# Where the second block's modulation vectors are summed: beside the first expert stage on VectorE, or partly by TensorE in 32-column tiles

## The reference, cut to what matters

```
mod = silu(c_2) @ ada_w_2 + ada_b_2            # (1024) @ (1024 x 6144)
sh1, sc1, gt1, sh2, sc2, gt2 = split(mod, 6)
xn   = rmsnorm(h, mix_norm_g) * (1 + sc1) + sh1
proj = xn @ w_in                               # queries, kv latent, index, shift and gate columns
...                                            # attention and a recurrent mixer
h = h + gt1 * (merged @ w_out)
xn2 = rmsnorm(h, moe_norm_g) * (1 + sc2) + sh2
h = h + gt2 * experts(xn2)                     # 32 experts, two per token
```

## Time and profile before

| | |
|---|---|
| time, median of 3 runs | 1485.1 us (1484.5 to 1487.49) |
| the profiled execution: its time, and its span | 1484.08 us, 1482.3 us |
| TensorE busy (matmul) | 1160.5 us, 78% of the span |
| VectorE, ScalarE, GpSimd busy | 36%, 18%, 3% |
| mean DMA rate over the span | 274 GB/s, 405.72 MB moved |
| first expert stage, first gate product to last down product | 258.6 to 514.8 us |

### The profile page before, as it was taken

One profiled execution on the slowest core, in us unless ns is written; L12 is line 12 of the kernel. 1 busy time (PEld: TensorE's weight loads), 2 busy tenths in 40 slices (PEclk: granted clock), 3 DMA queues, 4 the chain that ended last, 5 costly groups with the idle time before them and its releaser, 6 DMA issues. The chain is left out here.

```text
span 1482.3 us, 17064 instructions
## 1 busy us (share of the span) xinstructions
PE 1160.5 (78%) x6643; PEld 688.1 (46%) x6643; DVE 529.3 (36%) x1312; ACT 260.9 (18%) x654; POOL 41.6 (3%) x100
## 2 busy tenths in 40 slices
PE   2799688998899979788999997867666576566656
PEld 2688536443343347466777776543221221222212
DVE  5369573232233320665744446233011011010111
ACT  1233202111111220323522220011100100101000
POOL 0000000000000020000011100000000000000000
PEclk9999795999999979888999997878887887878888
DMA  9667954799999773022101101753999999999995
GB/s 346 233 253 263 413 191 183 296 428 426 427 430 427 298 270 118 17 98 74 57 2 57 58 16 44 281 234 139 421 422 422 422 422 422 422 422 422 422 421 232
DMA packets 78635, 405.72 MB, mean 274 GB/s; under 512 B 14231, under 2 KB 15444, under 8 KB 45812
## 3 DMA queue, kind: packets, MB, share of 16 engines
q1 hardware_dynamic: 78580, 404.98, 67.9%
HBM read 403.92 MB, written 1.05 MB: 273 GB/s over the span
## 5 line engine op out<-in xcount | busy, mean ns | idle before, releaser
L1049 PE MATMUL ps<-ring,hT_sb 128*32 128x512 f32 x768 | 117.0, 766 | 72.4 <-DMA ring<-in_expert_w_gate 42.1
L1412 PE MATMUL ps<-ring,hT_sb 128*64 128x512 f32 x448 | 117.6, 609 | 7.3 <-DMA ring<-in_expert_w_gate 5.5
L1049 PEld LDWEIGHTS ps<-ring,hT_sb 128*32 128x32 f32 x768 | 28.7, 136 | 154.4 <-issue 91.8
L1049 PE MATMUL ps<-side,hT_sb 128*32 128x512 f32 x256 | 42.6, 826 | 36.3 <-DMA side<-in_expert_w_up 18.5
L529 PE MATMUL ps<-hT_sb,ring 128*128 128x256 f32 x256 | 63.2, 398 | 7.7 <-ACT hT_sb L335 7.7
L1412 PEld LDWEIGHTS ps<-ring,hT_sb 128*64 128x64 f32 x448 | 36.4, 140 | 60.1 <-issue 52.9
L1061 PE MATMUL ps<-ring,tmp 128*32 128x512 f32 x384 | 49.6, 662 | 18.4 <-DMA ring<-in_expert_w_down 18.4
L1115 ACT ACTIVATE hT_sb<-ps,modc 128x128 f32<-128x128 f32 x72 | 27.1, 457 | 190.6 <-PE ps L1032 190.6
L1153 DVE TENSOR_TENSOR tmp<-ps,tmp 128x512 f32<-128x512 f32 x8 | 5.5, 692 | 153.4 <-ACT tmp L1123 153.4
L529 PEld LDWEIGHTS ps<-hT_sb,ring 128*128 128x128 f32 x256 | 48.8, 198 | 18.7 <-DVE hT_sb L328 7.7
L1622 PE MATMUL ps<-hT_sb,ring 128*128 128x256 f32 (+1 forms) x240 | 56.3, 392 | 1.4 <-DVE gate_rows L1801 1.4
(11 more groups left out here) (495 smaller groups left out, 1888.3 us busy)
## 6 DMA issues: line engine op xcount, KB each, us to landing
ring<-in_expert_w_gate SPq DMA_DIRECT2D x12, 4096.0 KB, 34.5
ring<-in_expert_w_up SPq DMA_DIRECT2D x12, 4096.0 KB, 34.7
ring<-in_expert_w_down SPq DMA_DIRECT2D x12, 4096.0 KB, 34.1
side<-in_ada_w SPq DMA_DIRECT2D x42, 1024.0 KB, 13.8
ring<-in_expert_w_down SPq DMA_DIRECT2D x16, 2048.0 KB, 17.5
ring<-in_expert_w_up SPq DMA_DIRECT2D x16, 2048.0 KB, 19.8
ring<-in_expert_w_gate SPq DMA_DIRECT2D x12, 2048.0 KB, 20.9
ring<-in_w_in SPq DMA_DIRECT2D x9, 2048.0 KB, 8.9
```

Source lines behind the costliest of these rows:

```text
L1049: last = pe.matmul(bank[es, :], xg[:, c, es], w[:, e, c % 4, :], start=(c == 0), stop=(c == KC - 1))
L1412: last = pe.matmul(bank[e * SLOTS:(e + 1) * SLOTS, :], xg[:, c, e * SLOTS:(e + 1) * SLOTS], dst(e, j, par)[:, c, :], start=(c == 0), stop= ...
```

## The change

Vectors 0 and 1 are now the ones that `ada2_side` loads (1 MiB for each pair of experts) and VectorE sums, in one 128x2048 multiply-add per pair. The other four (16 MiB) are loaded as eight chunks of 128 rows by 4096 columns, 2 MiB each, and multiplied on TensorE: the stationary operand is the chunk's column of `cond` repeated 32 times, so each matmul gives one half of a vector on 32 of the 128 partitions of an accumulator, four of them side by side in one bank. The gates' vectors are read as they lie; shift and scale are read with a step of eight floats. The chunks 0 to 3 are summed after the columns of vectors 0 and 1 and ahead of the transpositions, the chunks 4 to 7 after the index queries. SP issues four chunks and the four `w_in` loads, interleaved, after the expert loop and in its block; the others wait for the sums that free their buffers. The rest of the diff moves accumulators, turns the result rows into columns by four transpositions, clears 128x2048 of `acc` in place of 128x4096 at the routing, and drops the loads, sums and column products of the old placement.

```diff
-        def load_ada2(sp, pieces_): ...
-        def sum_ada2(v, i): ...
+        def ada2_at(k):
+            return (side[:, 0:CELL], side[:, CELL:2 * CELL], ring[:, 4 * CELL:5 * CELL], acc[:, 2 * D:6 * D],
+                    side[:, 0:CELL], side[:, CELL:2 * CELL], acc[:, 2 * D:6 * D], side[:, 0:CELL])[k]
+
+        def load_ada2(sp, k):
+            sp.dma_start(ada2_at(k), inp["ada_w_2"][0][k * P:(k + 1) * P, 2 * D:6 * D]).then_inc(sem(f"ada2_loaded{k}"), 16)
+
+        def sum_ada2(pe, k):
+            pe.wait_ge(sem(f"ada2_loaded{k}"), 16)
+            g1, sh, sc, g2 = [ada2_at(k)[:, m * D:(m + 1) * D] for m in range(4)]
+            parts = [[v[:, n * 512:(n + 1) * 512] for v in (g1, g2) for n in range(2)],
+                     [v.rearrange("p (q c) -> p c q", c=KC)[:, 4 * n:4 * n + 4, :] for v in (sh, sc) for n in range(2)]]
+            for b in range(2):
+                for j in range(4):
+                    last = pe.matmul(ps[2 + b][32 * j:32 * j + 32, :], cond[:, KC + k:KC + k + 1].broadcast_to((P, 32)),
+                                     parts[b][j], start=(k == 0), stop=(k == ADA2_CHUNKS - 1))
+            last.then_inc(sem("ada2_summed"), 1)
...
             # norms' block's predecessors: SP's load_ada2 calls, VectorE's sum_ada2 calls,
             # TensorE's ada_columns(pe, (0, 1), ...) and VectorE's fill_modc in the routing are gone
...
         def ada2_side(eng, it):
-            for j in range(2): ...          # two loads of 1 MiB and two multiply-adds a pair
+            ws, a = acc[:, 2 * D:4 * D], acc[:, 0:2 * D]
+            if eng is nc.sync:
+                if not isinstance(it, int) or it:
+                    eng.wait_ge(sem("ada2_row_used"), it)
+                eng.dma_start(ws, inp["ada_w_2"][0][bass.ds(it * P, P), 0:2 * D]).then_inc(sem("ada2_row_loaded"), 16)
+            else:
+                eng.wait_ge(sem("ada2_row_loaded"), 16 * it + 16)
+                eng.scalar_tensor_tensor(a, ws, cond[:, bass.ds(it + KC, 1)], a, ALU.mult, ALU.add).then_inc(
+                    sem("ada2_row_used"), 1)
...
+        def after_first(sp, last_pair):     # SP, still in the expert stage's block
+            (final norm's weights, as before)
+            load_ada2(sp, 0)
+            sp.wait_ge(sem("gate_used0"), last_pair)
+            p2_load(sp, 0, p2(0), w_cols(w_in, *pieces[0]))
+            load_ada2(sp, 1)
+            p2_load(sp, 3, p2(3), w_cols(w_in, *pieces[3]))
+            sp.wait_ge(sem("up_used0"), last_pair)
+            p2_load(sp, 1, p2(1), w_cols(w_in, *pieces[1]))
+            load_ada2(sp, 2)
+            sp.wait_ge(sem("ada2_row_used"), KC)
+            load_ada2(sp, 3)
+            sp.wait_ge(sem("down_used0"), last_pair)
+            p2_load(sp, 2, p2(2), w_cols(w_in, *pieces[2]))
+            sp.dma_start(kv_up, ...)
...
             # norms' block, SP: the w_in loads and kv_up are gone from here, krep and wi_w come first, then
+                for k, earlier in ((4, 0), (5, 1), (6, 3)):
+                    sp.wait_ge(sem("ada2_summed"), earlier + 1)
+                    load_ada2(sp, k)
+                sp.wait_ge(sem("x_ready"), 1)
+                (the two gate bias rows, now into g_b)
+                sp.wait_ge(sem("ada2_summed"), 5)
+                load_ada2(sp, 7)
...
             # norms' block, GpSimd:
+                pool.wait_ge(sem("ada2_summed"), 3)
...
             # norms' block, TensorE:
-                ada_columns(pe, (3, 4), 2, "modc_psum", perm=True)
+                ada_columns(pe, (0, 1), 0, "modc_psum")
+                for k in range(4):
+                    sum_ada2(pe, k)
                 hT_tensor(pe, 2)
...
                 last.then_inc(sem("pj_qi"), 1)
+                for k in range(4, ADA2_CHUNKS):
+                    sum_ada2(pe, k)
                 pe.wait_ge(sem("ki_loaded"), 80)
...
+                pe.wait_ge(sem("ada2_rows"), 2)     # ScalarE has copied ps[2], ps[3] into rows_g, rows_m
+                for c in range(4):
+                    last = pe.transpose(ps[7][:, c * P:(c + 1) * P], rows_m[:, c * P:(c + 1) * P], ident[:, :])
+                last.then_inc(sem("modc_psum"), 1)
...              (two times two matmuls of one row of ones against one row of rows_g, in place of ada_rows)
...
             # norms' block, VectorE, between the two norms:
+                v.wait_ge(sem("modc_psum"), FIRST_COLS + 2)
+                fill_modc(v, 3, 0, KC, ps[0][:, 0:KC], ps[0][:, KC:2 * KC], ...)
```

More of the change, by code:

```diff
@@ L225, in sum_ada2 @@
[L225 to L243, removed]
+        ADA2_CHUNKS = KC
@@ L486, in build, with fill_modc, shaped @@
         ada_at = [8 + sum(ADA_STEPS[:h]) for h in range(H + 2)]
[L488 to L493, removed]
+        def fill_modc(v, count, vec_scale, vec_shift, ps_shift, ps_scale, norm_col, ada_shift, ada_scale):
+            def shaped(a):
+                return a.rearrange("p (j c) -> p j c", j=2) if len(ps_shift.shape) == 3 else a
+            shift, scale = modc[:, vec_shift:vec_shift + KC], modc[:, vec_scale:vec_scale + KC]
+            v_step(v.tensor_tensor(shaped(shift), ps_shift, shaped(ada_shift), ALU.add))
+            v_step(v.tensor_tensor(shaped(scale), ps_scale, shaped(ada_scale), ALU.add))
+            v.scalar_tensor_tensor(scale, scale, 1.0, norm_col, ALU.add, ALU.mult).then_inc(sem("modc_ready"), 1)
             v.wait_ge(sem("modc_ready"), count)
@@ L1604, in p2_load, with p2 @@
             sp.dma_start(dst, src).then_inc(sem(f"p2_loaded{i % MIX_CELLS}"), 16)
+        def p2(i, kc=8, w=512):
+            return cell(i % MIX_CELLS, kc, w)
+        kv_up = cell(5)[:, 0:4, :].rearrange("p (c m) n -> p c (m n)", c=2)
+        def after_first(sp, last_pair):
+            sp.dma_start(g_b[:, 0, :], inp["norm_final"].rearrange("(a n) -> a n", a=1).broadcast_to((P, D))).then_inc(
+                sem("nf_loaded"), 16)
+            load_ada2(sp, 0)
[10 more added lines that the diff above has]
+            p2_load(sp, 2, p2(2), w_cols(w_in, *pieces[2]))
+            sp.dma_start(kv_up, inp["w_kv_up_2"][0].rearrange("(c p) n -> p c n", p=P)).then_inc(sem("kv_up_loaded"), 16)
+        route(0, 16, True)
+        if until > 4:
+            experts(0, 16, sides=ada2_side, afterwards=after_first)
+        if debug and until <= 5:
+            debug(nc, sem, locals())
+            return
+        give_back()
         SHIFT_NOW = 5
@@ L1661, in build @@
         lora = p2(LORA, 1, 4096)[:, 0, :]
-        kv_up = cell(5)[:, 0:4, :].rearrange("p (c m) n -> p c (m n)", c=2)
         M_STRICT, M_INCL = pos_t[:, 0:P], pos_t[:, P:2 * P]
@@ L1670, in _ @@
             def _(sp):
-                for i in range(4):
-                    p2_load(sp, i, p2(i), w_cols(w_in, *pieces[i]))
-                for i, m in enumerate((2, 5)):
-                    sp.dma_start(side[:, i * D:(i + 1) * D], inp["ada_b_2"][0:1, m * D:(m + 1) * D].broadcast_to((P, D))).then_inc(
-                        sem("gb2_loaded"), 16)
                 for r in range(4):
@@ L1800, in _ @@
                         a = g_b[:, i, n * 512:(n + 1) * 512]
-                        ins = v.tensor_tensor(a, ps[n][:, :], side[:, i * D + n * 512:i * D + (n + 1) * 512], ALU.add)
+                        ins = v.tensor_tensor(a, ps[n][:, :], a, ALU.add)
                     ins.then_inc(sem("g_out"), 1)
```

102 lines of the change are left out of this document (31 added, 71 removed).

## The result

| | before | after |
|---|---|---|
| median | 1486.18 us (4 runs, 1484.5 to 1487.49) | 1510.92 us (4 runs, 1502.56 to 1515.32) |
| ratio of the medians | 1 | 1.016, 95% interval 1.0115 to 1.0206 |
| profiled execution | 1484.08 us, span 1482.3 | 1515.32 us, span 1513.6 |

The changed kernel is slower by 24.7 us in the median. The forecast was 1498.4 us with a range to 1509: the sign was right, the size wrong, and the median lies 2 us outside the range.

The account below looks back on a forecast made before the run. Transfers were taken to pace the middle of the expert stage, then TensorE's path to set the time. Terms -12.5 + 5.8 + 6.5 + 7.1 + 4.0 + 1.6 + 0.8 = +13.3 on 1485.1 gave 1498.4 us, range 1484 to 1509.

Parts of the forecast that it names:

- The stage: First expert stage: less transfer per pair removes most waits at gate products, -12.5 us (bounds 9.3 to 16.4 returned).
- SP at the end of the stage: End of the expert stage: SP, held in kv_up's issue, finishes after VectorE, +5.8 us (bounds 0 and 8).
- The first four sums: Norms' block, sums of chunks 0 to 3 ahead of the transpositions on TensorE: +6.5 us (4.3 to 8).
- Strided reads: Rival: TensorE's reads with a step of eight floats cost, +3.5 us, 1502 us, up to 1505; chance 0.18.
- Sums 4 to 7: Norms' block, after the index queries: +7.1 us of sums, +4.0 waiting for chunk 7, +1.6 of half pace.
- the two terms: At the last sum: a wait of +4.0 us for chunk 7, then +1.6 us of half pace.
- Transpositions: Norms' block: four transpositions turning summed rows into columns, with their drain, +0.8 us.
- After the shifted products: Rest of the kernel: nothing is changed and no engine has slack to take the loss back.
- SP is not last: Rival: the queue takes w_in 2 earlier, the block begins 3.4 us after VectorE's last addition; 1492.6 us, chance 0.13.
- the queue is never late: Rival: loads pass the queue faster, so waits in stage, at its end and at chunk 7 go; 1483.1 us, chance 0.10.
- The move does nothing: Rival: stage gain and sums cancel, time within 3 us of 1485; chance 0.07.

Follow-up runs that it names:

- experiment 3: Kernel before with the second load and multiply-add of ada2_side left out (13 MiB a pair): 1470.63 us, ratio 0.9912.
- experiment 2: Changed kernel with only kv_up's load moved from SP's end of the expert stage to its start of the norms' block: 1495.91 us, ratio 1.0088.
- Experiment 1: Changed kernel with shift and scale vectors read straight instead of with a step of eight floats: 1503.43 us, ratio 1.0139.
- experiment 7: Changed kernel run once more, unaltered: 1511.28 us, ratio 1.0183.
- (4): Changed kernel with the gates' rows made by full 128x128 ones and all 128 partitions instead of one: 1510.0 us, ratio 1.0166.
- experiment 5: Changed kernel without the load of chunk 7, whose sum reads chunk 4 again: 1505.36 us, ratio 1.0142.
- (8): Changed kernel with the sums of chunks 4 to 7 left out of TensorE's list, chunk 7 not loaded: 1496.42 us, ratio 1.0078.
- (9): Changed kernel without its four transpositions of the shift and scale rows: 1510.23 us, ratio 1.0169.
- experiment 6: Changed kernel with kv_up loaded in the norms' block, all vectors read straight and chunk 7 not loaded: 1487.83 us, ratio 1.0028.
- version 11: Kernel before with vectors 2 and 5 loaded in eight late chunks and summed by VectorE during projections, ada2_side keeping 3 and 4: 1474.33 us, ratio 0.994.

## Why the prediction was right and wrong

**The stage: right.** -12.5 forecast, -12.1 measured, with the waits of pairs 4, 5 and 6 where they were said to be (forecast 0, 2.0 and 1.9; measured 0.16, 1.70 and 1.70). The first expert stage's pace by transfers was read correctly, and experiment 3 shows that most of its gain reaches the end.

**SP at the end of the stage: the step that failed most.** +5.8 forecast (at most 8), +13.0 measured. The step said that `kv_up`'s issue returns when w_in 2 is taken over, "which needs w_in 1 nearly gone: 515.8". That a held last issue holds the block is shown by experiment 2; the moment at which it returns is wrong by 8.0 us, and 13.0 lies 5 us beyond the step's own upper bound, which by itself carries the median past the range. I had counted rows, a chunk of `ada_w_2` as 128 of them, with a limit of some 1380 outstanding. The packets of the two traces refute that count: 64 rows of chunk 3 and the 1024 of w_in 2 were outstanding at 523.81, 1088 together, where before has 1463 to 1485 rows of 2 KB at its three returns (530.53, 536.0 and 541.3).

One count made afterwards fits better. If the rows of 16 KB count as four pieces of 4 KB, a chunk is 512, and a limit of 1280 puts the takeover of w_in 2 at the half of chunk 3. From my own queue times (past the norm's weights at 490.3, then 4.9 + 5.4 + 4.9 + 5.4 + 5.4 + 4.9 + half of 4.9) that is 523.65; it was 523.81. The same count gives half of chunk 1 (503.05; returned 503.07) and three quarters of w_in 3 (509.55; 509.67), and misses by 1.2 us at half of chunk 0 (492.75; 493.99). Nor does it give the rest: chunk 3 was taken over at 510.95 with, by this count, some 2100 pieces outstanding. So it is a fit to three of the held issues, not a rule that a run has tested, and how far the queue reaches stays open.

**The first four sums: +6.5 forecast, +8.0 measured.** The sums themselves took 12.6 us (533.72 to 546.31) where 9.3 were forecast: 2.9 of that is the strides, 0.4 a lower clock that lasted to about 539.3 and not 4.5 us. The columns ahead took 0.9 less, and the transpositions gave back 1.45 and not 0.5.

**Strided reads: the rival was true, at the price of its far end.** The step took 0 "since no row shows TensorE slowed by a step". No row showed the contrary either, and the nearest row, of another engine, did. Experiment 1 shows the strided half of the records at double the time at the upper clock, 0.98 us a chunk, and 6.8 us in all in the trace, above the 3.5 that the range allowed for it. The forecast named that case: "were the penalty a doubling, an estimate of mine, the sum would be 7 us more, 1505". Up to the shifted products, taking the strides away gave only 2.8 us (they start at 602.10 and not 605.84, and 0.91 of that is an earlier block), as the second half of it went into a longer wait.

The Trainium skill, page "SBUF — State Buffer", section "Door 1: The DMA port swizzle", has the rule of a penalty for each access that crosses to a new 16-byte line. The trace agrees with it for a TensorE moving operand at the upper clock: at a step of 32 bytes, 0.90 us for four records against 0.43. At the lower clock it shows hardly any penalty, 0.92 against 0.85.

**Sums 4 to 7: +12.7 forecast, +13.3 measured, by another split.** 11.1 of sums and strides, 2.17 of wait, no half pace. The wait was forecast 4.0 for sums of 1.77 us; with sums of 2.7 it is 2.17, and with straight ones it is 4.37 with 1.4 of half pace behind it, as the terms had it. So the two terms were right for a kernel without strides, and that their sum came close here is in part luck: the price that the strides added stands where the half pace and a part of the wait were forecast.

**Transpositions: +0.8, measured +1.0.**

**After the shifted products: "nothing is changed": false.** Some 7 us in the profiled execution (4.3 in experiment 7), from the clock, were in no term and in no rival. No row of before showed that this stretch keeps its clock when it is moved. Together: -12.1 + 13.0 + 8.0 + 0.1 + 13.3 + 1.6 + 7.0 = +30.9.

What lets the clock fall isn't settled. Shown, in one execution each, is what it is not: the strides (1), the held block (2), the one-partition rows (4), the wait (5), the sums 4 to 7 (8), the transpositions (9), each alone, and 1, 2 and 5 together (6). It falls in all eight kernels that have the sums on TensorE, always somewhere from the index key's last products to the gates' rows, and it also falls in version 11, whose list of products on that stretch is that of before, and not in before, twice. In 11 the block starts 12 us earlier than in before; in experiment 3, with the same list and an earlier block, it doesn't fall (L267 takes 1.96 and 1.98 us at 563.37 and 566.79). So the list alone doesn't decide it. Nor does the time since the clock last rose, unless half a microsecond of it matters: the rise comes at 530.9 and the rows 32.5 us later in experiment 3, at 531.7 and 33.0 us later in version 11. Whether it is that half microsecond or the load on the other engines (VectorE has eight more sums in 11), no run here tells apart. Not tried: the transposed sums in another order, or filler products on that stretch.

**Rivals "SP is not last" and "the queue is never late": false**, both by SP's timeline. **"The move does nothing": false** as it stood; experiment 6, with the mishaps removed, comes near it (+0.3%). Its trace shows that TensorE's own sums, 16.9 us of them on a path that had 2.2 us of idle time to give, use up the stage's gain by themselves.

## What to carry to other kernels

Before work moves off an engine that has slack for one whose path is unbroken, look for a stretch of the first engine where it idles beside the same cover: VectorE under the projections took the two gates' vectors without making TensorE wait, while TensorE paid 1.7 us for each straight chunk of four vectors, and 2.7 with the step. Let the last DMA issue of a block be one that returns at once, and count an issue as lasting until the transfers before it have made room; put one that is held into the next block's list. Keep the moving operand's step at one element, or measure the step that you need (only one and eight floats were measured here), and doubt a saved wait until the next thing it triggers (here a load into a freed buffer) has been costed.

## What the runs showed of the hardware beyond that

- A product of 128x512 float32 on a 32-column tile whose moving operand has a step of eight floats takes the same time at either clock. Groups of four tiles, by the starts of their records in after: at 1.2 GHz 0.85 us straight (533.72, 534.57, 535.42) and 0.92 strided (535.42, 536.35, 537.27); at 2.4 GHz 0.43 straight (541.24, 541.67) and 0.90 strided (541.67, 542.57). The step costs 8% at the lower clock and doubles the time at the upper.
- The gates' rows from one partition take 2.08 us for four records at 1.2 GHz, and 1.13 at 2.4 GHz in experiment 5; full rows take 1.96 at 2.4 GHz and 3.62 at 1.2.
- TensorE's clock fell to 1.2 GHz with the engine 2.00 of 2.00 us busy (after, 596 to 598) and held 2.4 GHz at 1.11, 1.43 and 0.62 of 2.00 (before, 576 to 582): the busy share of the moment doesn't tell it.
